# A mixer step on one core: output weights by ScalarE's queue, low parts and the last table part moved, the scan's decay by ScalarE, two pooled tiles per scan group

## What is computed

```python
def pool_mixer(u, buf, start_pos, pool_w, pool_scale):
    ...
    mixed = jnp.einsum('nlgc,gcd->nlgd', pooled, pool_w.astype(jnp.float32)).reshape(n, L, POOL_WIDTH)
    return mixed * pool_scale.astype(jnp.float32), z[:, -POOL_BUF:]

def ssm_mixer(u, h0_re, h0_im, ...):
    ...
    bu_re = jnp.einsum('nlgh,gph->nlgp', uf, bb_re)
    ...
    _, _, h_re, h_im = lax.associative_scan(complex_affine_combine, (ar, ai, bu_re, bu_im), axis=1)
    y = (jnp.einsum('nlgp,ghp->nlgh', h_re, c_re) - jnp.einsum('nlgp,ghp->nlgh', h_im, c_im) + d * uf)
    g = jax.nn.gelu(y)
    out = g * jax.nn.sigmoid(g @ glu_w + glu_b)

    mix = jnp.concatenate([pool_out, ssm_out], axis=-1).astype(x.dtype) @ prm['w_out']
    x = x + g1[:, None, :] * mix
    ... norm, router, 16 experts, final norm
```

## Time and profile before

| | us |
|---|---|
| median of three runs | 1182.48 |
| the profiled execution | 1183.54 |
| its span in the trace | 1181.7 |
| TensorE busy in the span | 1085.3 (92%) |
| VectorE busy | 776.4 (66%) |
| ScalarE busy | 508.1 (43%) |
| GpSimd busy | 283.1 (24%) |
| first instruction of `middle` on VectorE | 332.96 |
| first gate product (`glu 0`) | 467.53 |

### The profile page before, as it was taken

One profiled execution on the slowest core, in us unless ns is written; L12 is line 12 of the kernel. 1 busy time (PEld: TensorE's weight loads), 2 busy tenths in 40 slices (PEclk: granted clock), 3 DMA queues, 4 the chain that ended last, 5 costly groups with the idle time before them and its releaser, 6 DMA issues. The chain is left out here.

```text
span 1181.7 us, 18292 instructions
## 1 busy us (share of the span) xinstructions
PE 1085.3 (92%) x5541; PEld 804.8 (68%) x5542; DVE 776.4 (66%) x1276; ACT 508.1 (43%) x715; POOL 283.1 (24%) x347
## 2 busy tenths in 40 slices
PE   3799999999958899999999899999999999999991
PEld 2357777676546567787788556777877877778750
DVE  5556575747889973468887787655666555555384
ACT  5233242421132325446665243544555444455372
POOL 0046262616041000030000002333333333333212
PEclk9799999999988999999999999999999999999996
DMA  9834655557686449386765458887899777775597
GB/s 282 306 107 118 190 141 178 154 149 220 194 219 135 156 147 256 151 234 214 249 219 214 161 214 271 230 271 213 218 285 262 219 213 220 211 200 106 106 374 307
DMA packets 168381, 245.71 MB, mean 208 GB/s; under 512 B 65912, under 2 KB 124056, under 8 KB 165455
## 3 DMA queue, kind: packets, MB, share of 16 engines
q1 hardware_dynamic: 141697, 177.35, 47.0%
q0 software_dynamic: 14384, 49.53, 17.2%
q10 hardware_dynamic: 12246, 18.14, 4.6%
HBM read 169.36 MB, written 75.84 MB: 207 GB/s over the span
## 5 line engine op out<-in xcount | busy, mean ns | idle before, releaser
L126 PE MATMUL experts_psGU<-weights_we_hi,experts_x_hi 128*128 (+1 forms) x344 | 143.2, 416 | 2.9 <-issue 1.7
L128 PE MATMUL experts_psGU<-weights_we_lo,experts_x_hi 128*128 (+1 forms) x344 | 136.0, 395 | 0.0
L127 PE MATMUL experts_psGU<-weights_we_hi,experts_x_lo 128*128 (+1 forms) x344 | 135.8, 395 | 0.0
L126 PE MATMUL front_psM<-front_hT_hi,front_w_hi 128*128 128x512 f32 x256 | 106.5, 416 | 0.9 <-DVE front_hT_lo L1008 0.9
L127 PE MATMUL front_psM<-front_hT_hi,front_w_lo 128*128 128x512 f32 x256 | 101.2, 395 | 0.0
L128 PE MATMUL front_psM<-front_hT_lo,front_w_hi 128*128 128x512 f32 x256 | 101.1, 395 | 0.0
L2503 POOL DMA_INDIRECT acc_d<-experts_o_sb,experts_to_col x40 | 69.3, 1733 | 130.0 <-issue 73.1
L126 PEld LDWEIGHTS experts_psGU<-weights_we_hi,experts_x_hi 128*128 128x128 f32 x344 | 64.6, 188 | 28.8 <-issue 15.7
L2677 DVE TENSOR_TENSOR experts_x_lo<-experts_psX,experts_x_hi 128x1024 fp32r<-128x1024 f32 x42 | 51.4, 1224 | 37.5 <-ACT experts_x_hi L2567 37.5
L2667 DVE TENSOR_TENSOR weights_we_lo<-weights_we_raw,weights_we_hi (+1 forms) x64 | 75.4, 1219 | 0.0
L128 PEld LDWEIGHTS experts_psGU<-weights_we_lo,experts_x_hi 128*128 128x128 f32 x344 | 64.6, 188 | 15.5
(11 more groups left out here) (521 smaller groups left out, 2522.7 us busy)
## 6 DMA issues: line engine op xcount, KB each, us to landing
front_raw<-in_w_ada SPq DMA_DIRECT2D x32, 512.0 KB, 4.0
weights_we_raw<-in_exp_w_gate SPq DMA_DIRECT2D x16, 1024.0 KB, 5.9
weights_we_raw<-in_exp_w_up SPq DMA_DIRECT2D x16, 1024.0 KB, 12.5
weights_wd_raw<-in_exp_w_down SPq DMA_DIRECT2D x16, 1024.0 KB, 13.2
front_xraw<-in_x_prompt SPq DMA_DIRECT2D x4, 2048.0 KB, 9.9
front_raw<-in_w_ada SPq DMA_DIRECT2D x8, 1024.0 KB, 14.7
part_d<-middle_ev ACTq DMA_DIRECT2D x16, 512.0 KB, 3.6
middle_xt<-in_x_prompt SPq DMA_DIRECT2D x16, 512.0 KB, 4.8
```

What stands on the lines that cost most here:

```text
L126: pe.matmul(out, l_hi, r_hi, start=start, stop=False)
L127: pe.matmul(out, l_lo, r_hi, start=False, stop=False)
L128: return pe.matmul(out, l_hi, r_lo, start=False, stop=stop)
```

## The change

- `w_out`'s upper half is loaded by ScalarE's queue, behind its last stores of `u_d`, where SyncE loaded it after the last piece of `U`.
- SyncE's list: `ada_second` comes ahead of `last_load`, and each `last_load(m)` comes one group later; the last one follows the last block. The store of the table piece 6 moves from the last block's group 6 to its group 7. The load of the first two `mraw` tiles comes ahead of the last stores and no longer waits for the store of `tail`.
- VectorE's `kk_diag(7)` moves behind 28 of the 32 copies (it was behind 8).
- The low parts `wp_lo` 0 and 1 are made at the end of `front`; 2 and 3 stay in `middle`, behind `m_split(0)`.
- `rho` is filled by ScalarE, behind its first two `m_split`s; only its first column stays with VectorE.
- `SEQ`: `p1 5`, `p1 7` and `p1 9` come ahead of `y 1`, `y 2` and `y 3`, so that each scan group has two `p1`. ScalarE makes `m_split(5)` behind the outputs of `y 0`. VectorE makes `m_split(2q + 2)` between the two halves of a scan group and `m_split(2q + 3)` inside the second half.
- ScalarE's `gw_hi` moves from behind `p1 9` to behind `p1 10`.

```diff
-                def out_weights():
-                    sp.wait_ge(s["mm_done"], KD * NBLK)
-                    for i in range(2):
...
                             for i in range(STEP if b + 1 < NBLK else STEP // 2):
                                 sp.dma_start(u_v[i, gs, :, c0:c0 + CB],
                                              ust[:, m % 2, i * CB:(i + 1) * CB]).then_inc(ust_out[m % 2], 16)
-                            if b + 1 == NBLK:
-                                last_load(m)
-                            if b + 1 == NBLK and m + 1 == KD:
-                                out_weights()
                         if 8 * b + m + 2 < 8 * NBLK:
                             ada_second(8 * b + m + 2)
+                        if b + 1 == NBLK and m in (QH, QH + 2, QH + 3):
+                            last_load(m if m == QH else m - 1)
...
+                last_load(KD - 1)
                 sp.wait_ge(s["tail_ok"], 1 + QH * NBLK)
...
+                sp.wait_ge(s["p_out"], 16 * QH * NBLK)
+                sp.wait_ge(s["a2_ev"], ADA2_N)
+                for t in range(2):
+                    sp.dma_start(mraw[:, t], mix_d[0:HALF, t * P:(t + 1) * P].rearrange("(q p) n -> p q n", p=P)
+                                 ).then_inc(T.m_in[t], 16)
                 mod_store(ADA2_N - 1)
                 kk_store(NCK - 1)
...
+                    if b + 1 == NBLK:
+                        act.wait_ge(s["mm_done"], KD * NBLK)
+                        for i in range(2):
+                            c = slice(i * BLK, (i + 1) * BLK)
+                            act.dma_start(wp_raw[:, :, c], a["w_out"][0].rearrange("(k p) n -> p k n", p=P)[:, 0:QH, c]
+                                          ).then_inc(wp_in, 16)
                     table(kk_fill(2 * b + 1), P, 4)
                 act.wait_ge(wp_in, 32)
...
-                state_inputs(0, 8)
+                state_inputs(0, 2 * PAIRS - 4)
                 kk_diag(NCK - 1)
-                state_inputs(8, 2 * PAIRS)
+                state_inputs(2 * PAIRS - 4, 2 * PAIRS)
+                for i in range(2):
+                    c = slice(i * W4, (i + 1) * W4)
+                    dve.wait_ge(wp_h, i + 1)
+                    dve.tensor_tensor(wp_lo[:, :, c], wp_raw[:, :, c], wp_hi[:, :, c].bitcast(F32), ALU.subtract
+                                      ).then_inc(wp_l, 1)
...
-       ("p1", 4), ("y", 1), ("p1", 5), ("p1", 6), ("y", 2), ("p1", 7), ("p1", 8), ("y", 3), ("fin", 0), ("p1", 9),
+       ("p1", 4), ("p1", 5), ("y", 1), ("p1", 6), ("p1", 7), ("y", 2), ("p1", 8), ("p1", 9), ("y", 3), ("fin", 0),
        ("p1", 10), ("p1", 11), ("p1", 12), ("glu", 0), ("p1", 13), ("glu", 1), ("p1", 14), ("glu", 2), ("p1", 15),
...
-SPLITS = {2: [], 3: [], 4: [5, 6]}
+SPLITS = {2: [], 3: [], 4: [6]}
...
+                act.copy(rho[:, :, 1:], sm[:, 6, :].unsqueeze(2).broadcast_to([P, PAIRS, HC])).then_inc(s["rho_ok"], 1)
...
                     elif what == "y":
                         outputs(n)
+                        if n == 0:
+                            m_split(5)
...
-                out_lo(0)
-                out_lo(1)
                 m_split(0)
                 out_lo(2)
                 out_lo(3)
                 m_split(1)
-                dve.tensor_copy(rho[:, :, 1:], sm[:, 6, :].unsqueeze(2).broadcast_to([P, PAIRS, HC]))
-                ch.link(dve.memset(rho[:, :, 0:1], 0.0))
+                dve.memset(rho[:, :, 0:1], 0.0).then_inc(s["rho_ok"], 1)
+                dve.wait_ge(s["rho_ok"], 2)
...
+                        scan(q, half, 2 * q + 3 if half == 1 else None)
+                        if half == 0:
+                            m_split(2 * q + 2)
+                            continue
...
-                for t in (9, 10, 11):
+                for t in (10, 11):
                     m_split(t)
```

More of the change, by code:

```diff
@@ L270, in front @@
         s = {n: k.sem("fr_" + n) for n in names}
-        wp_in, wp_h = T.wp_in, T.wp_h = [k.sem("fr_" + n) for n in ("wp_in", "wp_h")]
+        wp_in, wp_h, wp_l = T.wp_in, T.wp_h, T.wp_l = [k.sem("fr_" + n) for n in ("wp_in", "wp_h", "wp_l")]
         T.m_in = [k.sem(f"m_in{i}") for i in range(2)]
@@ L472, in _ @@
                             cl_store(2 * b)
-                        if m == 6:
-                            if b + 1 == NBLK:
-                                vb_store(NCK - 1)
+                        if m == 6 and b + 1 == NBLK:
+                            vb_store(NCK - 1)
+                        elif m == 6:
                             kk_store(2 * b)
@@ L487, in _ @@
                 sp.wait_ge(s["tail_out"], 16)
-                sp.wait_ge(s["p_out"], 16 * QH * NBLK)
-                for t in range(2):
-                    sp.dma_start(mraw[:, t], mix_d[0:HALF, t * P:(t + 1) * P].rearrange("(q p) n -> p q n", p=P)
-                                 ).then_inc(T.m_in[t], 16)
                 sp.wait_ge(s["cl_out"], 16 * NCK)
@@ L1251, in middle @@
         psG, psR, psL, psL2 = psX[:, 2, :], psX[:, 3, 0:P], psX[:, 3, P:2 * P], psX[:, 2, P:P + CR]
-        names = ("smp_in", "x_fill", "x_evac", "t_zero", "t_in", "dve_step", "pool_step",
-                 "pooled", "h_ready", "h_head", "row_out", "fin_ok", "wp_l",
+        names = ("smp_in", "x_fill", "x_evac", "zeroed", "t_in", "dve_step", "pool_step",
+                 "pooled", "h_ready", "h_head", "row_out", "fin_ok", "rho_ok",
                  "pmhi", "pmlo", "p1_mm", "p1_ev", "gw_in", "gw_h", "gw_l", "gb_in", "ws_h", "ws_l", "ghi", "glo",
                  "g_mm", "sg_done", "mo_done", "mhi", "mlo", "rows_in", "rw_in", "mm", "tmp",
-                 "x2_done", "sq", "ms", "rt", "h2_done", "h_t", "h_ev", "r_mm", "r_ev", "l_t", "lg_done", "r_zero")
+                 "x2_done", "sq", "ms", "rt", "h2_done", "h_t", "h_ev", "r_mm", "r_ev", "l_t", "lg_done")
         s = {n: k.sem("m_" + n) for n in names}
@@ L1913, in out_lo @@
                     dve.wait_ge(wp_h, i + 1)
[L1914 to L1917 removed]
+                    tt(wp_lo[:, :, c], wp_raw[:, :, c], wp_hi[:, :, c].bitcast(F32), ALU.subtract).then_inc(wp_l, 1)
                 m_split(0)
@@ L1921, in _ @@
                 m_split(1)
-                dve.tensor_copy(rho[:, :, 1:], sm[:, 6, :].unsqueeze(2).broadcast_to([P, PAIRS, HC]))
-                ch.link(dve.memset(rho[:, :, 0:1], 0.0))
-                late = 2
+                dve.memset(rho[:, :, 0:1], 0.0).then_inc(s["rho_ok"], 1)
+                dve.wait_ge(s["rho_ok"], 2)
                 for q in range(PAIRS // QP):
                     for half in range(2):
-                        scan(q, half, 3 if q == 0 and half == 1 else None)
-                        if half == 1:
-                            if q == 0:
-                                dve.wait_ge(s["x_evac"], at["h0"] + 1)
-                                for i in range(2):
-                                    ins = dve.tensor_copy(H[:, i, :, 0:NSEQ].rearrange("p k b -> p b k"), h0[:, i])
-                                ins.then_inc(s["h_head"], 1)
-                            dve.sem_inc(s["h_ready"], 1)
-                        if q == 0 and half == 1:
-                            late += 1
-                        elif late < 9:
-                            m_split(late)
-                            late += 1
+                        scan(q, half, 2 * q + 3 if half == 1 else None)
+                        if half == 0:
+                            m_split(2 * q + 2)
+                            continue
+                        if q == 0:
+                            dve.wait_ge(s["x_evac"], at["h0"] + 1)
+                            for i in range(2):
+                                ins = dve.tensor_copy(H[:, i, :, 0:NSEQ].rearrange("p k b -> p b k"), h0[:, i])
+                            ins.then_inc(s["h_head"], 1)
+                        dve.sem_inc(s["h_ready"], 1)
                 p8 = [PW[:, i, STEP:STEP + 1, :].broadcast_to([P, NSEQ, PAIRS]) for i in range(2)]
```

26 lines of the change are left out of this document (12 added, 14 removed).

## The result

The changed kernel takes 1185.1 us in the median of its runs against 1182.3 us for the kernel before on the same chip: ratio 1.0023, 95% interval 1.0013 to 1.0033, so it is **slower by about 2.7 us**, where I had forecast 6.5 us faster and a range that ended at 1180.5. The profiled execution took 1187.28 us, 2.2 above that median, with a span of 1185.5 us (1181.7 before); losses read from its trace come out larger than the 2.7 us. The first gate product starts at 471.13 us instead of 467.53, and from there on the two traces run alike (714.4 us to the end of the span, 714.2 before); so the whole loss, and some gain that was eaten up, lies between 300 and 471 us.

What follows compares the result with a forecast made beforehand. VectorE's preparation and scan chain behind the barrier were taken as the bound, then TensorE from `fin` on; the first gate product 6.5 us earlier (461.0 against 467.5) gave 1182.5 - 6.5 = 1176.0 us, range 1171.0 to 1180.5.

Steps and rivals of the forecast that it cites:

- The load of the second product's weights: First stage: load issued seven us earlier, TensorE's 2.2 us wait goes; state copies run 310.95 to 325.3.
- The last pieces of `U`: End of `front`: pieces travel beside the output weights; cost taken as 0, bounds -1 (the clock) and +4 us.
- the second of the list: Rival, chance 0.15: weights' packets hold up the last `U` pieces, barrier at 331 to 333, loss 2.5 to 4.5 us.
- The weights themselves: End of `front`: output weights issued 7.5 us sooner, landing at 324.2; four casts end at 328.1.
- Barrier to scan: Start of `middle`: scan starts 4.4 us behind the barrier, at 332.9, 10 us earlier than before.
- The decay on ScalarE: Start of `middle`: ScalarE's fill of `rho` takes 1.94 us and is hidden; 1 us cost if it took 4.13.
- The clear of `T`: Scan's first products: GpSimd's clear now runs beside them; priced at 0, bound +3.5 us.
- The scan chain: VectorE's scan: 92.8 us against 90.2, with a 3.6 us wait for high part 5, ending at 425.7, 7.4 earlier.
- Behind the scan: ScalarE awaits tile 11 until 435.5, `fin` ends 7.1 us later at 442.6; gate begins at 461.0, 6.5 earlier.
- the front's edits: Everything up to the scan's start, which was to come 10 us earlier, at 332.9.
- the order: Second stage with two `p1` per scan group: of 10 us won at the scan's start, 6.5 remain at the gate.

Runs made afterwards that it cites:

- e4: Changed kernel with the last-but-one kk store and last state store moved behind the last load of `U` on SyncE's queue: 1.0027 of the kernel before, +3.2 us.
- g2: Changed kernel with high part 5 and tile 11's load early, ScalarE handing over the output weights only once the last `U` piece landed: 0.9920 of before.
- e1: Changed kernel with both output weight loads back on SyncE's queue, right behind the last piece of `U`: 0.9989 of the kernel before, -1.3 us.
- e5: Changed kernel with output weights on SyncE's queue behind the last `U` piece, tile 11's load early and high part 5 early: 1169.7 us, 0.9879 of before.
- g1: Changed kernel with the old second-stage order and the output weights on SyncE's queue behind the last `U` piece: 0.9915 of the kernel before, -10.1 us.
- e2: Changed kernel with the load of mixed tile 11 moved ahead of SyncE's wait for the final states: 0.9976 of the kernel before, -2.8 us.
- f1: Changed kernel with its second-stage order put back as before, front edits kept: 0.9946 of the kernel before, -6.4 us.
- f2: Kernel before with the new second-stage order alone: 1.0059 of the kernel before, +7.0 us.
- e3: Changed kernel with ScalarE's high part 5 made behind high part 4, ahead of the outputs of `y 0`: 0.9975 of the kernel before, -3.0 us.
- g5: Changed kernel with tile 11 and high part 5 early, half the output weights by ScalarE early, half by SyncE behind `U`: 0.9898 of before.

## Why the prediction was wrong

The time was 9.2 us off (2.7 slower, forecast 6.5 faster); at the first gate product of the trace it is 10.1 us (461.0 against 471.1). Step by step:

- **The load of the second product's weights: right.** The wait is gone, and the copies start at 309.76 (forecast 310.95). The 1.2 us more are the -1 of my bounds: TensorE kept its clock (1.00 from 310 to 312 us, where it was 0.50 behind the wait).
- **The last pieces of `U`: the step that failed.** "Below I take 0 for that, and as bounds -1 (the clock) and +4." It was 5.8 us at the barrier (334.3 against 328.5): 3.9 us of wait, and 2.95 because TensorE came back at the lower clock (6.73 us for the 32 products that took 3.78 in e4), less the 1.2 that the copies were ahead. Both halves of the mistake can be seen in my text. In the rival I wrote against it that the weights begin only after the stores that the pieces wait for; but the pieces are issued after those stores land, so this is just what puts the weights ahead of them. And the bound of +4 held the wait without the clock behind it, although show such a fall behind a stop of 3.1 us. Moving the weights to ScalarE's queue brought no bandwidth (9.0 us from issue to the first cast in g2, 8.5 to 9.1 by SyncE's queue in e1, e5 and g1), only the right to go first, and 6.3 and 8.1 us for the piece against 3.0 to 4.1 are the price. This agrees with the rule that I quoted from the Trainium skill, "DMA: Bandwidth & Descriptors", section "Issuing engines are not separate DMA queues", that another queue saves only issue time. I had the case as a rival (the second of the list, though the text above it says third), at 0.15 and with a loss of 4.5 at most; it deserved far more. But this step is not the whole miss: with it mended (e1) the time is 4.0 us better, of the 9.2.
- **The weights themselves: right** (casts from 323.08, forecast 324.2), but of no use: they are cast by 326.96, and VectorE still copies until 331.06. From SyncE's queue they are cast 2.2 to 2.9 us later, counted from ScalarE's last stores of `u_d` (16.2 to 16.9 us behind them in e5, g1 and e1, 14.0 in the changed kernel), and the barrier still comes earlier.
- **Barrier to scan: right** (4.3 us, forecast 4.4). The decay on ScalarE took 1.90 us and is hidden. The clear of `T` beside the scan's first products cost nothing, as priced: the product at 338.59 took 0.69 us inside GpSimd's clear, 337.97 to 341.49. That agrees with the page "SBUF — State Buffer", section "Who interferes with whom", of the Trainium skill.
- **The scan chain: mechanism right, size 2.5 us short.** VectorE waited 5.86 us for high part 5, not 3.6. In e1, where `y 0` does not wait for `T`, it is 4.03; where it waits 1.40, 1.95 and 2.34 us (e4, e2, changed), it is 4.25, 5.66 and 5.86. So 0.4 us is my sum, and nearly all of the rest is a late `y 0` (26.4 us after the scan's start, 24.8 in e1), by a wait for `T` that I had not seen: its loads went out at 350.35, 8.3 us after the issue of a 512 KB store of zeros that reads `T`, where it was 5.0 us before. (Where high part 5 is made ahead of `y 0`, as in g2, or wanted later, as in f1, waits of 2.8 and 2.7 us for `T` leave the chain at 89.5 and 90.1.) I had started `y 0` with `h_ready(0)` although the scan, 4.3 us earlier than before, was bound to come close to a transfer that I had not moved (347.34 before). f2 shows the same wait without `T`: 5.53 us, where `y 0` begins 25.9 us after the scan's start, straight behind TensorE's products for the pooled tiles.
- **Behind the scan: mechanism right, 2.0 us short.** ScalarE got tile 11 9.1 us behind the scan's end (forecast 9.8), and from this release `fin` took 9.1 us (forecast 7.1). Half of the difference is again the clock (0.66, against the 1.00 of e2): the first two groups of products take 4.1 us where they need 2.2 at full clock, and I had counted 0.8 for that; what the other 0.9 is stays open. The gate's own operand added 0.5 (TensorE's wait at 471.13).
- **By parts:** I gave the front's edits 10 us, and they are worth 10.1 with the weights behind the piece (g1) and 6.4 with them ahead of it (f1). I gave the order a cost of 3.5 us (10 - 6.5), and it cost 7.0. I had seen both of its waits, and did not ask whether each could be removed by moving one line (e2 and e3 do it), nor whether an order that brings two waits of 4 to 7 us is a gain at all.

**What stays open.** Why the store of zeros took 5.0 to 8.5 us from kernel to kernel wasn't tried. Behind the barrier two 512 KB stores of partial sums now lie in the same stretch, one before; but e3 has two as well, and there the zeros took 6.1 us and `y 0` did not wait for `T`. Nor is it known why the clock fell behind some of TensorE's stops and not behind others of the same length (last section).

## What to carry to other kernels

In these runs a transfer that was put on an idle engine's queue did not get a lane of its own: it got a place ahead of what was issued after it. Before moving a large load forward, list the small loads that will be issued while it is in flight and who stands waiting for them, and let the small ones go first. When a sum contains a stop of TensorE, put the slow clock behind it into the bounds (here it cost 2.95 us, 1.9 us and, in e4, nothing); and when an edit brings a wait that a line moved a few places in a queue would remove, move the line before judging the edit.

## What the runs showed of the hardware

- A load of 256 KB took 3.0 to 4.1 us with none of the weights ahead of it, also where 2 MB followed 0.4 to 1.1 us behind it (before, f2, e1, e5, g1); 6.3 us with 1 MB handed over 3.3 us ahead of it on another queue (g5); and 7.6 to 8.7 us with 2 MB handed over 3.4 to 3.7 us ahead.
- After stops of 3.9 and 6.25 us TensorE's granted clock was 0.58 in the next 7 us and 0.66 in a stretch of 10 us with the stop in it. The length of a stop alone did not tell: behind 3.36 us in e4 the clock stayed at 1.00, behind 3.35 us in g1 it was 0.50 for the next 5.7 us, and behind 2.75 us in f1 0.51 and 0.57 in the next 1.7 and 2.0 us. Two stops of 1.2 and 1.1 us left it at 1.00 in e2; two of 1.2 and 0.8 us in e5 were followed by 0.57 over 4 us (0.89 in the 16 us around them), and in the kernel before one of 2.2 us, for the second product's weights, by 0.50 over 2 us.
